# Paged sample attention joined with the mLSTM gate tiles and output products, in a one-core decode step of a hybrid mLSTM and MoBA layer

## The reference, cut to what matters

```python
q_m, k_m, v_m, o_m, if_pre, q_a, k_a, v_a, g_m, g_a = split(xn @ W['w_in'])     # xn = RMSNorm(x)
h_m = ...   # mLSTM output, 8 heads x 128
h_a = moba_attention(q_a, pos, k_all, v_all)   # 8 heads x 128; sample: 8 pages x 128 past tokens + its own
u = sigmoid(g_m) * (h_m @ W['w_proj_m']) + sigmoid(g_a) * (h_a @ W['w_proj_a'])
x = x + u @ W['w_out']
```

## Time and profile before

| | |
|---|---|
| median of three runs | 2368.83 us |
| the profiled execution: its own time / its span | 2376.53 / 2374.9 us |
| sample attention, K steps of batch 0 to the last d_h | about 580.8 to 850 us |
| gates and products, to the last product | about 850 to 1177.8 us |
| TensorE busy, share of the span; mean granted clock | 91%; 0.939 |
| VectorE, ScalarE, GpSimd busy | 51%, 34%, 2% |
| DMA: bytes, mean rate | 380 MB, 160 GB/s |

### The profile page before, as it was taken

One profiled execution on the slowest core, in us unless ns is written; L12 is line 12 of the kernel. 1 busy time (PEld: TensorE's weight loads), 2 busy tenths in 40 slices (PEclk: granted clock), 3 DMA queues, 4 the chain that ended last, 5 costly groups with the idle time before them and its releaser, 6 DMA issues.

```text
span 2374.9 us, 40363 instructions
## 1 busy us (share of the span) xinstructions
PE 2169.8 (91%) x16438; PEld 2022.0 (85%) x16438; DVE 1203.9 (51%) x1392; ACT 795.9 (34%) x994; POOL 58.4 (2%) x76
## 2 busy tenths in 40 slices
PE   4999997998767789999999987899999999999997
PEld 4989986997444469999899866799999999999997
DVE  3364445443333336665635544666564446665543
ACT  3343322433222223333323432433333333333333
POOL 0010101110000000000000000000000000000000
PEclk7998996999788879999999998899999999999999
DMA  6244542451576675454444534245445555454453
GB/s 194 78 130 150 178 137 83 152 182 58 206 283 252 243 249 175 141 170 148 142 142 137 166 132 151 93 155 177 157 149 155 161 191 167 151 177 159 158 159 113
DMA packets 304706, 380.03 MB, mean 160 GB/s; under 512 B 6003, under 2 KB 278547, under 8 KB 303971
## 3 DMA queue, kind: packets, MB, share of 16 engines
q1 hardware_dynamic: 300530, 365.72, 47.2%
q0 software_dynamic: 4112, 13.41, 1.8%
HBM read 368.58 MB, written 10.52 MB: 160 GB/s over the span
## 4 chain that ended last, share of the span: by engine, by line
PE 71%; PEld 13%; DVE 5%; DMA 3%; SPq 3%; issue 3%; ACT 2%; PEldq 0%; DVEq 0%; POOL 0%; ACTq 0%; POOLq 0%
PE bank L1613 15%; PE bank L1614 15%; PE bank L1617 15%; PE bank L1627 7%; PE bank L1631 5%; PE bank L2067 4%; PE bank L2066 4%; PE bank L2071 4%; PEld bank L1613 3%; PEld bank L1617 3%; PEld bank L1614 3%; DMA raw<-cache_v_dram 2%; PEld bank L1922 1%; PEld bank L1923 1%; PE bank L1624 1%
## 5 line engine op out<-in xcount | busy, mean ns | idle before, releaser
L982 DVE TENSOR_TENSOR w_lo<-raw,w_hi 128x2048 fp32r<-128x2048 f32 (+1 forms) x289 | 622.8, 2156 | 676.4 <-ACT w_hi L590 671.4
L1613 PE MATMUL bank<-xn_hi,w_hi 128*128 128x288 f32 x3152 | 876.0, 305 | 58.5 <-DVE xn_lo L1022 26.1
L1614 PE MATMUL bank<-xn_lo,w_hi 128*128 128x288 f32 x3152 | 868.7, 301 | 0.0
L590 ACT ACTIVATE w_hi<-raw 128x2048 fp32r<-128x2048 f32 (+1 forms) x289 | 518.0, 1794 | 887.7 <-PE bank L1617 623.5
L1613 PEld LDWEIGHTS bank<-xn_hi,w_hi 128*128 128x128 f32 x3152 | 610.9, 194 | 69.3 <-issue 53.5
L1614 PEld LDWEIGHTS bank<-xn_lo,w_hi 128*128 128x128 f32 x3152 | 610.1, 194 | 0.1
L1617 PE MATMUL bank<-xn_hi,w_lo 128*128 128x288 f32 x3152 | 451.9, 296 | 0.0
L1617 PEld LDWEIGHTS bank<-xn_hi,w_lo 128*128 128x128 f32 x3152 | 430.4, 189 | 0.0
L2066 PE MATMUL bank<-f_hi,w_hi 128*128 128x288 f32 x704 | 191.4, 296 | 0.0
L2067 PE MATMUL bank<-f_lo,w_hi 128*128 128x288 f32 x704 | 190.8, 297 | 0.0
L1631 PE MATMUL bank<-consts,raw 128*128 128x128 f32 (+1 forms) x656 | 115.7, 313 | 40.7 <-DVE d_qpad L1271 13.3
(11 more groups left out here) (358 smaller groups left out, 1767.7 us busy)
## 6 DMA issues: line engine op xcount, KB each, us to landing
raw<-w_in_dram SPq DMA_DIRECT2D x44, 2048.0 KB, 8.3
raw<-w_ffn_gate_dram SPq DMA_DIRECT2D x22, 2048.0 KB, 8.1
raw<-w_ffn_up_dram SPq DMA_DIRECT2D x22, 2048.0 KB, 8.1
raw<-w_ffn_down_dram SPq DMA_DIRECT2D x32, 1408.0 KB, 6.5
raw<-cache_k_dram SPq DMA_DIRECT2D x64, 512.0 KB, 5.1
raw<-cache_v_dram SPq DMA_DIRECT2D x64, 512.0 KB, 5.0
raw<-w_out_dram SPq DMA_DIRECT2D x8, 2048.0 KB, 8.2
raw<-w_proj_m_dram SPq DMA_DIRECT2D x8, 1024.0 KB, 5.4
```

Of the source, the lines that this page charges most:

```text
L590: nc.scalar.activation(like(wh[ph.half(c)], src), src, ACT.Copy).then_inc(hi_ready, 1)
L982: nc.vector.tensor_tensor(like(wl[ph.half(c)], src), src, like(wh[ph.half(c)], src).bitcast(F32), ALU.subtract).then_inc(slot_read[ph.slot ...
L1613: mm(out, wh[half][:, k, :], rh[:, k, 0:n], start=k == 0, stop=False)
L1614: mm(out, wh[half][:, k, :], rl[:, k, 0:n], start=False, stop=False)
```

## The change

Sample attention, the `g_m` tiles and the `h_m` products become one loop over the 8 batches (phase `p_gm`, iteration b handles batch b and output features 256b to 256b+255). The `g_a` tiles and `h_a` products follow in a loop of their own (`p_ga`). In iteration b TensorE does: 16 matmuls of the first `g_m` tile; the row transposes of batch b-1; the 16 K steps, each with two more matmuls of that first tile between its transposes and the scores of the step before; the own scores; the second `g_m` tile; the first `h_m` half tile (24 matmuls); the transposes of the probabilities of the same batch b; the second `h_m` half tile; the V products of batch b.

```diff
@@ tensor
+            def d_batch(b, first):
+                gm_part(b, 0, 16)
+                if not first:
+                    rows_t(b)
+                pe.wait_ge(d_q, b + 1)
+                for n in range(17):
+                    if n < 16:
+                        if n % 4 == 0:
+                            pe.wait_ge(kv_landed[r], b * 64 + 32)
+                        ... 4 x tr(B[2 + n % 2][...], ring(r)[...])
+                        last.then_inc(d_tr, 1)
+                        gm_part(b, 16 + 2 * n, 18 + 2 * n)
+                    if n:
+                        pe.wait_ge((d_kta, d_ktd)[(n - 1) % 2], b * 8 + ((n - 1) // 2 + 1))
+                        ... 4 scores; after the first of steps 4, 8, 12, 16: kv_read[n // 4 - 1] + 1
+                        last.then_inc(d_ss, 1)
+                pe.wait_ge(d_h, b + 1)
+                ... own scores .then_inc(d_sc, 1)
+                tile(p_gm, b, 0, 1, 1)
+                half_tile(p_gm, b, 0, hmh, hml, pm_read, b * 2 + 1)
+                hold(pe, d_pn, b + 1)
+                ... 9 transposes of DP .then_inc(d_ptr, 1)
+                half_tile(p_gm, b, 1, hmh, hml, pm_read, b * 2 + 2)
+                pe.wait_ge(d_ptc, b + 1)
+                for r in range(4):
+                    pe.wait_ge(kv_landed[r], b * 64 + 64)
+                    ... V products of 2 pages .then_inc(kv_read[r], 1)
+                ... own values .then_inc(d_pv, 1)
+            def ga_body(i, first):
+                for j in range(2):
+                    tile(p_ga, i, 0, j, j)
+                    if first and not j:
+                        rows_t(NB)
+                if first:
+                    pe.wait_ge(d_lo, 1)
+                for j in range(2):
+                    half_tile(p_ga, i, j, hah, hal, slot_read[p_ga.slot(1)], p_ga.reads(i, 1, j + 1))
```

The half tiles go through banks 0 and 1 like the others and have no `drain`. Pages get a ring of four regions of two pages (1 MB) in `raw1` and `raw2`, weights of `g_m` keep `raw0`, and `w_proj_m` (1 MB per iteration) has a buffer `pm_w` of its own:

```diff
@@ sync
+            with sp.Fori(0, NB - 1) as b:
+                gm_load(b + 1)
+                for r in range(4):
+                    pages(b, r, a["cache_v"], b * 2 + 1)      # waits kv_read[r]
+                pm_load(b + 1)                                 # waits pm_read
+                for r in range(4):
+                    pages(b + 1, r, a["cache_k"], b * 2 + 2)
+            ...
+            with sp.Fori(1, 8) as i:
+                ga_load(i)        # 2 MB, raw0, after both lo of iteration i - 1
+                pa_load(i)        # 1 MB, raw1
@@ scalar, one batch
+                hi x2 for g_m(b); rows_out(b) (hrow of batch b - 1); 8 copies to KTb[0]
+                gate_evac(p_gm, b, 0); pm_hi(b, 0)
+                wait d_sm; exp of DP; gate_evac(p_gm, b, 1); pm_hi(b, 1); wait d_ptr; 3 copies to PT
@@ vector, one batch
+                qpad; lo x2 for g_m(b); 8 copies to KTb[1], rows_in(b) after the third
+                ... the same choice of blocks, table and maximum as before
+                pm_lo(b, 0); wait d_p; reciprocal; scale DP; pm_lo(b, 1)
+                gate_sig(p_gm, b, 0, 2)      # + 1 and reciprocal on 128x576
+                2 x: wait gemm_done; U[2b + j] = bank * sg[j]
@@ vector, gates and products of h_a
+            def ga_tail(i, j):
+                dve.wait_ge(gemm_done, p_ga.conv(i, 3 + j))
+                dve.wait_ge(x_u, i * 2 + (j + 1))
+                dc.run(nc.vector.tensor_tensor(ut[:], G[p_ga.bank(2 + j)][:, 0:NT], sg[:, j, :], ALU.mult))
+                dc.sync()
+                nc.vector.tensor_tensor(U2[:, ds(i * 2 + j, 1), :], U[...], ut[:].unsqueeze(1), ALU.add).then_inc(x_u, 1)
+                nc.vector.engine_nop().then_inc(evac_done[p_ga.bank(2 + j)], 1)
+            def ga_body(i, first):
+                for j in range(2):
+                    if not first:
+                        lo(p_ga, i, 0, j, src256(p_ga.slot(0), j))
+                        ga_tail(i - 1, j)
+                for j in range(2):
+                    lo(p_ga, i, 1, 2 + j, pa_src(j))
+                    gate_sig(p_ga, i, j, 1)
@@ vector, end
             lo(p_wo, 0, 0, 0, src256(p_wo.slot(0), 0))
-            mx_tail(7, 1)
             for q in range(4):
+                if q == 3:
+                    ga_tail(7, 0)
+                    ga_tail(7, 1)
                 dve.wait_ge(x_uhi, q + 1)
                 ... xl of four feature groups
+            dve.wait_ge(x_back, 16 * 8)
```

`U` needs room that is live during the attention's stage, so it takes the place of `xT` (the residual x, 2.36 MB). GpSimd stores `xT` to DRAM after the first transposes and reads it back two feature groups at a time as the final `U2` groups get ready:

```diff
@@ gpsimd
             load_c(0)
+            gp.wait_ge(tp_even, 5)
+            gp.wait_ge(tp_odd, 4)
+            gp.dma_start(x_rows, xT[:]).then_inc(x_out, 16)
...
+            with gp.Fori(0, 8) as i:
+                hold(gp, x_u, i * 2 + 3)
+                gp.dma_start(xT[:, ds(i * 2, 2), :], x_rows[:, ds(i * 2, 2), :]).then_inc(x_back, 16)
```

More of the change, by code:

```diff
@@ L455, in _ @@
             sp.wait_ge(d_pg, 16)
[L457 to L473, removed]
             def wt(name):
@@ L477, in _, with gm_load @@
             w_pm, w_pa, w_out = wt("w_proj_m"), wt("w_proj_a"), wt("w_out")
[L478 to L482, removed]
+            def gm_load(b):
+                load(p_gm, b, 0, full(p_gm, 0), w_in[:, :, ds(b * 256 + W_GM, 256)])
@@ new lines, in ga_load, with pa_load @@
+            def ga_load(i):
+                load(p_ga, i, 0, full(p_ga, 0), w_in[:, :, ds(i * 256 + W_GA, 256)])
+            def pa_load(i):
+                load(p_ga, i, 1, full(p_ga, 1)[:, 0:H], w_pa[:, :, ds(i * 256, 256)])
+            ga_load(0)
+            for r in range(4):
+                pages(NB - 1, r, a["cache_v"], 2 * NB - 1)
+            for r in range(4):
+                sp.wait_ge(kv_read[r], 2 * NB)
+            pa_load(0)
+            with sp.Fori(1, 8) as i:
+                ga_load(i)
+                pa_load(i)
@@ new lines, in gate_sig, with pm_lo @@
+            def gate_sig(ph, i, t, n):
+                for b in range(t, t + n):
+                    dve.wait_ge(evac_done[ph.bank(b)], ph.evacs(i, b) + 1)
+                dc.run(nc.vector.tensor_scalar(sg[:, t:t + n, :], sg[:, t:t + n, :], 1.0, None, ALU.add))
+                dc.sync()
+                dc.run(nc.vector.reciprocal(sg[:, t:t + n, :], sg[:, t:t + n, :]))
+                dc.sync()
+            def pm_lo(b, j):
+                dve.wait_ge(hi_ready, p_gm.conv(b, 3 + j))
+                nc.vector.tensor_tensor(like(wl[p_gm.half(2 + j)], pm_src(j)), pm_src(j),
+                                        like(wh[p_gm.half(2 + j)], pm_src(j)).bitcast(F32), ALU.subtract).then_inc(pm_read, 1)
@@ new lines, in gm_part @@
+            def gm_part(b, first, end):
+                half, out = p_gm.half(0), G[p_gm.bank(0)][:, 0:NT]
+                for n in range(first, end):
+                    if n == 0:
+                        pe.wait_ge(hi_ready, p_gm.conv(b, 1))
+                        wait(pe, evac_done[p_gm.bank(0)], p_gm.evacs(b, 0))
+                    if n == 2 * KT:
+                        pe.wait_ge(slot_read[0], p_gm.reads(b, 0, 1))
+                    if n < 2 * KT:
+                        last = mm(out, wh[half][:, n // 2, :], (xh, xl)[n % 2][:, n // 2, :], start=n == 0, stop=False)
+                    else:
+                        last = mm(out, wl[half][:, n - 2 * KT, :], xh[:, n - 2 * KT, :], start=False, stop=n == 3 * KT - 1)
+                if end == 3 * KT:
+                    last.then_inc(gemm_done, 1)
@@ new lines, in half_tile @@
+            def half_tile(ph, i, j, rh, rl, read, at_least):
+                half, out, bank = ph.half(2 + j), G[ph.bank(2 + j)][:, 0:NT], ph.bank(2 + j)
+                pe.wait_ge(hi_ready, ph.conv(i, 3 + j))
+                wait(pe, evac_done[bank], ph.evacs(i, 2 + j))
+                for k in range(H):
+                    mm(out, wh[half][:, k, :], rh[:, k, :], start=k == 0, stop=False)
+                    mm(out, wh[half][:, k, :], rl[:, k, :], start=False, stop=False)
+                pe.wait_ge(read, at_least)
+                for k in range(H):
+                    last = mm(out, wl[half][:, k, :], rh[:, k, :], start=False, stop=k == H - 1)
+                last.then_inc(gemm_done, 1)
@@ L1930, in _ @@
+            ga_body(0, True)
+            with pe.Fori(1, 8) as i:
+                ga_body(i, False)
             for j in range(4):
```

368 lines of the change are left out of this document (186 added, 182 removed).

## The result

The changed kernel takes 2297.97 us (median of four runs, 2287.91 to 2302.91) against 2368.93 us (2368.3 to 2374.9) for the kernel before (a fourth run has joined its three): a ratio of 0.969, 95% interval 0.9652 to 0.9727. Its profiled execution took 2295.74 us with a span of 2294.1 us; that of before took 2376.53. The profiled difference is 80.8 us, the one between the medians 71.0; the forecast was 77.4.

The account below looks back on a forecast made before the run. Attention starved TensorE on pages and halved its clock; the gates and products were nothing but TensorE. Terms 1.4 + 42.7 + 298.2 + 175.4 + 14.3 = 532.0 us against 609.4, 77.4 less, median 2291, range 2266 to 2328.

Parts of the forecast that it names:

- Batches: Joined loop: 40.3 us of TensorE work a batch, 42.6 with waits and lost clock; seven take 298.2, batch 0 42.7.
- The K wait: Joined loop, before K step 0: next batch's K pages land late, 1.5 us a batch, bounds 0 to 5.1.
- the clock: After each TensorE stall: 0.8 us lost to half clock, the middle between nothing and 1.65 us.
- Start: Start of the joined loop: batch 0 begins 1.4 us later than the first transposes did, because w_hi is made first.
- The h_a loop: Gates and products of h_a: 19.2 us an iteration, seven stalls of 2.25 us awaiting bank 0, plus 0.8 clock each: 175.
- The end: After the last product: the first w_out tile ends at about 14.3 us, where it was 12.4 before.
- x out and back: Store of x: 0, at most 10 us; its reload before the second w_out tile: 0, at most 4.5, paid once.
- the stalls vanish: Joined and h_a loops: K pages land in time and the clock stays, 22 us less, 2269; chance 0.13.
- the DMA queue binds: Joined loop: 11.5 MB a batch at 250 GB/s takes 46.1 us, giving 2316; chance 0.13.
- the change fills nothing: Joined loop: matmuls behind waiting transposes leave idle time as it was, 78 us more, 2369, no change; chance 0.04.
- The slower case: K steps run at half clock, 0.97 us more a step, 124 us in all, 2415; chance 0.05.
- The covers: Joined loop: matmuls hide the softmax (7.8 us under 9.6), VectorE's gates, and the V pages (wanted 14 us later).

Follow-up runs that it names:

- the exchange of two lines: Changed kernel with ga_tail(i - 1, j) ahead of the next tile's remainder lo on VectorE in the h_a loop: 2275.39 us, ratio 0.9583.
- the changed kernel's second execution: The changed kernel measured again with no edit, beside other kernels: 2295.96 us, ratio 0.9689.
- the edits: Changed kernel with ga_tail ahead of lo, the whole first g_m tile ahead of the K steps, and ga_tail(7, 0) ahead of the w_out remainder: 2260.5 us.
- the short pages: Changed kernel with only 16 of a page's 128 tokens moved in each transfer: 2280.97 us, ratio 0.9624; same edit in the kernel before: 2333.55 us.
- the kernel with the tile ahead: Changed kernel with the whole first g_m tile ahead of the K steps, no matmuls between them: 2285.57 us, ratio 0.9639.
- the kernel with less cover: Changed kernel with the first h_m half tile moved behind the transposes of the probabilities: 2304.96 us, ratio 0.9722.

## Why the prediction was right

The likeliest case came true, 7 us from the median and inside the range. Point by point, over the stretch of 82.2 us gained where 77.4 were forecast:

- **Batches.** TensorE's own work was put at 40.3 us and is 40.09 (the period without page waits). The K wait was put at 1.5 and is 1.3 in the mean, seven times (8.8 us; doing without it gave 1.48 a batch). The step that failed is the clock: 0.8 us for each stall was the middle of two bounds, and in this loop it is the lower one, nothing, at a granted clock of 1.00. Eight batches take 332.3 us (579.52 to 911.85) instead of 340.9: 8.6 less.
- **Start.** TensorE's first matmul comes 0.5 us later than it did, counted from the end of the prompt's attention, where I had 1.4: 0.9 less.
- **The h_a loop.** The chain w_lo, x_tmp, x_u ahead of a tile's start was forecast, and the exchange of two lines shows it. Six of the seven stalls are 2.2 us, where 2.25 were put. Here the clock's 0.8 is near the mean of two cases: three iterations take 21.7 us at full clock and three 23.2 with a stretch at half. Most of the miss is the first iteration, 25.65 us (922.85 to 948.50) instead of 22.25. Its stall is 3.44 us: w_hi starts 1.2 us later than its free buffer would let it, because its 2 MB of w_in have not landed, and I had said that the transfers bind nothing there. The half clock behind the stall costs another 2.8 us (the first 32 matmuls of the tile take 7.11 us, 934.99 to 942.10, for 4.27 at full clock). In the changed kernel's second execution the same stall of 3.43 us cost 1.6 in clock. The other six iterations add 1.3 us. The loop takes 180.2 us (911.85 to about 1092) instead of 175.4: 4.8 more.
- **The end.** 14.2 us from the last product to the end of the first w_out tile, forecast 14.3.
- **x out and back.** 0 on TensorE's path as the trace stands, with VectorE waiting 1.94 us for it.

These differences, -8.6 - 0.9 + 4.8 - 0.1, give the 4.8 us by which the stretch did better. That the median came out 7 above the forecast lies elsewhere. I carried over from before that its profiled execution stood 7.7 us above the median; that of the changed kernel stands 2.2 below its own, and the part of the program behind the stretch took 3.2 us more in it. So two misses of 8.6 and 4.8 us cancel in part inside the stretch, and the four runs of the changed kernel lie 15 us apart: that the median is only 7 us off says less than the rows of the single terms do.

**The rivals.** That the stalls vanish (2269) is not what happened, but the edits reach it and go beyond: 2260.5. That the DMA queue binds (2316) falls with the short pages: the period moves by the K wait alone. That the change fills nothing (2369) falls with the windows. The slower case, K steps at half clock, falls with the steps of 1.20 us: 0.41, 0.44 and 0.35 us from one start to the next. The granted clock is 1.00 over 288 us in which, in the kernel with the tile ahead, long runs of K steps are 0.58 us transposes of every 0.94. By the rule in the Trainium skill, TensorE: Matmul & The Clock Gate, Part 4: PE-mode transpose, that a transpose doesn't count as busy, they would have fallen to half clock; for runs of these float32 transposes with scores between them the trace disagrees, and the measurement decides. No run here has transposes alone.

**The covers.** The one over the softmax is shown by taking 3.2 us of it away. The one over the V pages is seen only in the trace (no wait for cache_v), and so is that over the gates on VectorE.

## What to carry to other kernels

Joining a stage that starves TensorE with one that is nothing but TensorE was worth 82.2 us of the profiled stretch here: the idle time on V pages is gone, and the joined loop runs at full clock. But filler placed behind a waiting instruction on an in-order engine fills nothing: put it ahead of the wait.

Then follow each PSUM bank to the instruction that frees it, and ask what stands ahead of that on its engine; if it waits, directly or not, for the engine that wants the bank, move the release ahead. Here that was two lines exchanged, for 20.6 us.

## What the runs showed of the hardware that I had not expected

- A stall does not have one price in clock. Seven stalls of up to 1.5 us, each after 40 us of dense work, and eight more of 1.5 us in the kernel with less cover, cost nothing beyond themselves. Those of 2.2 us in the h_a loop were followed by a stretch at half clock in three iterations and not in the other three, 1.5 us or nothing, with the same instructions around them; the first one, of 3.4 us, cost 2.8 us in one execution and 1.6 in another. What decides is open.
- The queue and the DMA engines sustain 281 GB/s at a share of 0.80 beside a TensorE that is busy 39.69 of 41 us, with the landing of a page hardly longer than before (5.3 us instead of 5.1). With an eighth of the page bytes the period moved by 1.48 us, little more than the K wait, so the load on the DMA engines cost the stage no more than that.
- A page's bytes are only about half of its price in the old attention: with an eighth of the bytes the waits on pages fell from 48.5 to 21.1 us, and the kernel's time by 35.
